# Residual rows in a seven-product down-projection: loaded by single tiles, a kept product, and their additions on GpSimd

## The reference

```python
def conv_ffn(h, w_up, conv_w, conv_b, w_down):
    u = causal_dwconv(h @ w_up, conv_w, conv_b)
    gate, val = jnp.split(u, 2, axis=-1)
    return (jax.nn.silu(gate) * val) @ w_down        # (1024, 2816) @ (2816, 1024)
...
x = x + concatenate([tok, xa]) @ w_out               # x_mid, kept in DRAM
x = x + conv_ffn(rms_norm(x, ffn_norm[i]), ...)      # the residual addition
h = rms_norm(x, mix_norm[i + 1])                     # what the next layer reads
```

## Time and profile before

| | |
|---|---|
| three runs | 2541.0, 2546.72, 2546.8 us |
| profiled execution, its own time | 2542.37 us |
| its span | 2540.6 us |
| PE busy | 2436.7 us (96%) |
| DVE busy | 1731.4 us (68%) |
| ACT busy | 1030.8 us (41%) |
| POOL busy | 194.6 us (8%) |
| mean DMA rate | 101 GB/s |

### The profile page before, as it was taken

The page is one execution under the profiler, slowest core; times in us unless marked ns, Lnnn a source line. Parts: engine busy times, 40 slices in busy tenths (PEclk is TensorE's granted clock), DMA queues, the critical chain, the costliest instruction groups (busy, mean ns, idle before and its releaser), DMA issues. The chain is left out here.

```text
span 2540.6 us, 32368 instructions
## 1 busy us (share of the span) xinstructions
PE 2436.7 (96%) x11700; PEld 2056.7 (81%) x11700; DVE 1731.4 (68%) x2934; ACT 1030.8 (41%) x2118; POOL 194.6 (8%) x269
## 2 busy tenths in 40 slices
PE   7999979999999998998999999998999999999898
PEld 7998757888888886777889889887888888887777
DVE  4432564479998987885553562463769989988895
ACT  6433443344444443335434442333334444443332
POOL 1010121000000000001212022122000000000000
PEclk9999988999999999999999999999999999999999
DMA  4231112222222247643102011212532222227653
GB/s 147 89 88 22 48 70 58 84 68 83 92 83 75 91 154 273 228 138 128 55 17 80 34 34 42 59 34 80 173 107 83 83 75 92 83 85 256 250 176 140
DMA packets 207349, 257.72 MB, mean 101 GB/s; under 512 B 38184, under 2 KB 141592, under 8 KB 207192
## 3 DMA queue, kind: packets, MB, share of 16 engines
q1 hardware_dynamic: 203032, 255.65, 30.6%
q10 hardware_dynamic: 4160, 0.02, 0.1%
HBM read 206.54 MB, written 49.09 MB: 101 GB/s over the span
## 5 line engine op out<-in xcount | busy, mean ns | idle before, releaser
L52 PE MATMUL psum<-f_T_lo 128*128 128x512 f32 x616 | 246.8, 401 | 31.0 <-DVE f_T_lo L654 29.3
L53 PE MATMUL psum<-f_T_lo 128*128 128x512 f32 x616 | 242.2, 393 | 0.0
L54 PE MATMUL psum<-f_T_lo 128*128 128x512 f32 x616 | 241.8, 393 | 0.0
L52 PE MATMUL psum<-w_hi,hT_hi 128*128 128x512 f32 x576 | 229.3, 398 | 3.9 <-DVE w_lo L1415 2.2
L54 PE MATMUL psum<-w_hi,hT_lo 128*128 128x512 f32 x576 | 226.3, 393 | 0.0
L53 PE MATMUL psum<-w_lo,hT_hi 128*128 128x512 f32 x576 | 226.1, 393 | 0.0
L52 PEld LDWEIGHTS psum<-f_T_lo 128*128 128x128 f32 x616 | 117.0, 190 | 68.2 <-DVE f_T_lo L654 40.9
L52 PEld LDWEIGHTS psum<-w_hi,hT_hi 128*128 128x128 f32 x576 | 124.8, 217 | 22.1 <-issue 3.5
L54 PEld LDWEIGHTS psum<-w_hi,hT_lo 128*128 128x128 f32 x576 | 125.0, 217 | 17.8
L53 PEld LDWEIGHTS psum<-w_lo,hT_hi 128*128 128x128 f32 x576 | 125.1, 217 | 16.6
L52 PE MATMUL psum<-hT_hi,f_up_hi 128*128 128x512 f32 x352 | 137.4, 390 | 0.4 <-DVE f_up_lo L593 0.4
(11 more groups left out here) (412 smaller groups left out, 6053.1 us busy)
## 6 DMA issues: line engine op xcount, KB each, us to landing
raw<-in_ffn_w_up_dram SPq DMA_DIRECT2D x88, 512.0 KB, 4.7
activations<-f_act SPq DMA_DIRECT2D x44, 512.0 KB, 2.6
f_up_pieces<-activations SPq DMA_DIRECT2D x38, 512.0 KB, 4.1
w_raw<-in_b_w_in_dram SPq DMA_DIRECT2D x18, 1024.0 KB, 6.1
f_up_pieces<-in_ffn_w_down_dram SPq DMA_DIRECT2D x20, 512.0 KB, 4.9
x_between<-XY SPq DMA_DIRECT2D x16, 512.0 KB, 5.3
XY<-x_between SPq DMA_DIRECT2D x4, 2048.0 KB, 15.4
f_up_pieces<-activations SPq DMA_DIRECT2D x28, 256.0 KB, 3.9
```

The costliest lines, as they stand in the source:

```text
L52: nc.tensor.matmul(out, lhs_hi, rhs_hi, start=start, stop=False)
L53: nc.tensor.matmul(out, lhs_hi, rhs_lo, start=False, stop=False)
L54: return nc.tensor.matmul(out, lhs_lo, rhs_hi, start=False, stop=stop)
```

## The change

- `load_rows` loads single tiles (512 KB): tiles 4 to 7 behind the loads of groups 5, 7, 9 and 10, tiles 0 to 3 behind those of 14, 16, 18 and 20. The store of the last activations moves from group 8 to group 12.
- POOL makes all additions of `k1` and `k7` to the rows: four 128x512 after step 0; four 128x512 and four 128x1024 (both halves of `x21` and `x22` with `k7` read twice) after `second_sums`; then four 128x512 that add the product which step 1 left in PSUM. That product is now copied out by ACT (`keep_second`, `p2_copy`, in the room of `conv_out`). `third_first` waits for all 16.
- `begin.low_parts` goes from DVE to POOL, between POOL's first four additions and the rest.
- `second_sums` and `third_second` each become four operations of 128x1024 in place of eight of 128x512.
- `taps_of` of the last chunk: value half behind the lows of group 3, gate half behind those of group 6; `silu` behind group 7, `multiply` behind group 8.
- `load_right` has four places instead of two and is issued up to four groups ahead. In step 3 the order of the norm's parts on ACT, DVE and PE is another, and four of its DVE operations come behind the last lows.

```diff
-Q, X11A, U, X11B, XU, X21P, X2P, X12F = 0, 4, 8, 16, 20, 32, 36, 44
+Q, U, X21P, X2P, X12F = 0, 4, 8, 12, 16
@@ raw_single
-                return up.pieces[:, 2 * (n % 2), :]
+                return (up.pieces[:, 2, :], up.pieces[:, 6, :], up.room[:, 0, FIRST], up.pieces[:, 0, :])[(n - LAST) % 4]
@@
+        p2_copy = [conv_out[i // 2][:, (i % 2) * HALF:(i % 2 + 1) * HALF] for i in range(4)]
...
+        def both(x):
+            return x.unsqueeze(1).broadcast_to([P, 2, HALF])
+        def halves(x):
+            return x.rearrange("p (h n) -> p h n", n=HALF)
@@ sync
-                sp.wait_ge(b_split, parts_until(LAST + g - 1))
-                sp.dma_start(raw_single(LAST + g), down_rows[2 * g + 1, :, SECOND]).then_inc(e_loaded[(LAST + g) % 2], 16)
-            def load_rows(i):
+                sp.wait_ge(b_split, parts_until(LAST + g - 3 if g >= 4 else LAST - 2 + max(0, g - 1)))
+                sp.dma_start(raw_single(LAST + g), down_rows[2 * g + 1, :, SECOND]).then_inc(e_loaded[g % 4], 16)
+            def load_rows(t):
                 sp.wait_ge(p_done, ALL)
-                sp.dma_start(X[:, 4 * i:4 * i + 4, :], ...)
+                sp.dma_start(X[:, t, :], x_mid[t * P:(t + 1) * P, :]).then_inc(x_loaded[t // 4], 16)
@@
-                if n == 8:
+                if n in (5, 7, 9, 10):
+                    load_rows({5: 4, 7: 5, 9: 6, 10: 7}[n])
+                if n == PAIRS + 1:
                     store_act(FC - 1)
-                    for i in (1, 0):
-                        load_rows(i)
+                if n in (14, 16, 18, 20):
+                    load_rows((n - 14) // 2)
@@ scalar
+            def keep_second():
+                act.wait_ge(prod_done, FC)
+                for i in range(4):
+                    act.wait_ge(out_done, 12 + i + 1)
+                    nc.scalar.activation(p2_copy[i], psum[:, 4 + i, :], ACT.Copy).then_inc(p2_copied, 1)
...
+                if n == 2 * PAIRS + 1:
+                    keep_second()
                 high_parts(n)
-                if n == 4:
+                if n == 7:
                     silu(FC - 1)
...
-                if begin and n == 2 * PAIRS + 1:
+                if begin and n == 2 * PAIRS + 3:
                     act.wait_ge(b_split, parts_until(2 * PAIRS))
                     begin.high_parts(act)
@@ vector
             def second_sums():
                 for i in range(4):
                     dve.wait_ge(out_done, 8 + i + 1)
-                    dve.wait_ge(added, X11A + 4)
-                    add(k1[:, i, :], k1[:, i, :], psum[:, i, :])
-                    add(k7[:, i, :], k7[:, i, :], psum[:, i, :])
-                for i in range(4):
-                    dve.wait_ge(out_done, 12 + i + 1)
-                    add(x11[i], x11[i], psum[:, 4 + i, :])
+                    dve.wait_ge(added, Q + 4)
+                    dve.wait_ge(rows_added, 4)
+                    k_both = halves(h_room[1][:, DH + i, :])
+                    add(k_both, k_both, both(psum[:, i, :]))
...
             def third_first():
                 for i in range(4):
-                    dve.wait_ge(added, XU + 12)
+                    dve.wait_ge(rows_added, 16)
...
+                pieces = X[:, i:i + 5:4, SECOND]
+                add(pieces, pieces, both(psum[:, 4 + i, :]))
...
-                if PAIRS + 2 <= n < PAIRS + 6:
-                    rows_first(n - PAIRS - 2)
-                if 2 * PAIRS + 2 <= n < 2 * PAIRS + 6:
-                    rows_second(n - 2 * PAIRS - 2)
-                if begin and n == 2 * PAIRS + 6:
-                    begin.low_parts(dve)
...
+            for g in range(5, PAIRS):
+                lows(LAST + g)
+                if norm and g in (5, 7, 9):
+                    norm.dve_gain(dve, (g - 5) // 2)
+                elif norm:
+                    norm.dve_low(dve, (g - 6) // 2)
@@ gpsimd
+            def row_add(out, x):
+                nc.gpsimd.tensor_tensor(out, out, x, ALU.add).then_inc(rows_added, 1)
+            pool.wait_ge(x_loaded[1], 64)
+            for i in range(4):
+                pool.wait_ge(k1_copied, i + 1)
+                row_add(x11[i], k1[:, i, :])
+            if begin:
+                begin.low_parts(pool)
+            pool.wait_ge(x_loaded[0], 64)
+            for i in range(4):
+                pool.wait_ge(added, U + i + 1)
+                row_add(x12[i], k1[:, i, :])
+                row_add(halves(X[:, i, :]), both(k7[:, i, :]))
+            for i in range(4):
+                pool.wait_ge(rows_added, 12)
+                pool.wait_ge(p2_copied, i + 1)
+                row_add(x11[i], p2_copy[i])
@@ tensor
+                elif step == 2 and which == 1:
+                    pe.wait_ge(p2_copied, i + 1)
...
-                if norm and 2 <= g < 6:
-                    turn_first(g - 2)
+                if norm and g in (2, 3, 4, 6):
+                    turn_first((2, 3, 4, 6).index(g))
```

More of the change, by code:

```diff
@@ L514, in _ @@
                 act.wait_ge(b_made, 3 * LAST)
-            for g in range(4):
+            for g in range(PAIRS):
+                if norm and g >= 4:
+                    if g == 4:
+                        square(0)
+                    if g == 5:
+                        scale(0)
+                        square(1)
+                    if g == 6:
+                        scale(1)
+                        norm.act_high(act, 0)
+                        square(2)
+                    if g == 7:
+                        scale(2)
+                    if g == 8:
+                        norm.act_high(act, 1)
+                        square(3)
+                    if g == 9:
+                        scale(3)
+                    if g == 10:
+                        norm.act_high(act, 2)
                 high_parts(LAST + g)
             if norm:
[L518 to L533, removed]
-                act.wait_ge(b_split, parts_until(LAST + PAIRS))
[L535 to L540, removed]
+                norm.act_high(act, 3)
+                act.wait_ge(b_split, parts_until(LAST + PAIRS))
+                square(4)
+                square(5)
+                scale(4)
+                scale(5)
+                square(6)
+                norm.act_high(act, 4)
+                scale(6)
+                square(7)
+                norm.act_high(act, 5)
+                scale(7)
+                norm.act_high(act, 6)
+                norm.act_high(act, 7)
         @block.vector
@@ L797, in _ @@
                 dve.wait_ge(act_stored, 16 * FC)
[L798 to L807 removed]
+            for g in range(5, PAIRS):
[4 more added lines that the diff above has]
+                    norm.dve_low(dve, (g - 6) // 2)
+            if norm:
+                norm.dve_gain(dve, 3)
+            for i in range(4):
                 rows_last(i)
+                if norm and i == 1:
+                    norm.dve_low(dve, 3)
             if norm:
[L810 to L814 removed]
+                for t in range(4, TT):
                     norm.dve_gain(dve, t)
                     norm.dve_low(dve, t)
[L818 to L820 removed]
+        @block.gpsimd
+        def _(pool):
+            def row_add(out, x):
[11 more added lines that the diff above has]
+                row_add(halves(X[:, i, :]), both(k7[:, i, :]))
+            for i in range(4):
+                pool.wait_ge(rows_added, 12)
+                pool.wait_ge(p2_copied, i + 1)
+                row_add(x11[i], p2_copy[i])
+            if norm:
                 for t in range(TT):
@@ L875, in wait_bank @@
                     pe.wait_ge(k1_copied, i + 1)
+                elif step == 2 and which == 1:
+                    pe.wait_ge(p2_copied, i + 1)
                 else:
-                    pe.wait_ge(added, {(1, 1): Q + i + 1, (2, 0): U + 2 * i + 2, (2, 1): X11B + i + 1, (3, 0): X21P + i + 1}[step, which])
+                    pe.wait_ge(added, {(1, 1): Q, (2, 0): U, (3, 0): X21P}[step, which] + i + 1)
             def turn_first(t):
-                pe.wait_ge(added, X2P + (8 if t % 2 else 4))
+                pe.wait_ge(added, X2P + (4 if t % 2 else 2))
                 norm.pe(pe, t)
@@ L908, in _ @@
                 last.then_inc(out_done, 1)
-                if norm and i == 2:
-                    pe.wait_ge(added, X12F + 2)
-                    norm.pe(pe, 4)
             if norm:
+                pe.wait_ge(added, X12F + 2)
+                norm.pe(pe, 4)
                 pe.wait_ge(norm.low, begin.TILES)
@@ L1349, in high_parts, with low_parts @@
             self.nc.scalar.activation(self.hi[kh], self.raw(kh), ACT.Copy).then_inc(self.high, 1)
-    def low_parts(self, dve):
+    def low_parts(self, pool):
         for kh in range(2):
-            dve.wait_ge(self.high, kh + 1)
-            self.nc.vector.tensor_tensor(self.lo[kh], self.raw(kh), self.hi[kh].bitcast(F32), ALU.subtract).then_inc(self.split, 1)
+            pool.wait_ge(self.high, kh + 1)
+            self.nc.gpsimd.tensor_tensor(self.lo[kh], self.raw(kh), self.hi[kh].bitcast(F32), ALU.subtract).then_inc(self.split, 1)
```

47 lines of the change are left out of this document (10 added, 37 removed).

## The result

The changed kernel takes 2550.56 us (median of 11 runs, 2546.62 to 2555.14), the kernel before 2542.95 on the same chip: a ratio of 1.0029, 95% interval 1.0019 to 1.0039 (the ratio is of the means, without one run of the kernel before that took 3465.47 us). That is 7.6 us or 0.3% slower where 2520 and faster were forecast. The profiled execution took 2553.04 us, its span 2551.2, which is 10.6 over the span before.

A forecast was written before the change was run, and what follows sets the result against it. PE is busiest, its down-projection waiting for DVE's low parts. Terms sum to -9.4 us in f0 and -14.9 in f1, together -24.3 on 2542.4: 2518, put at 2520 against the median; range 2502 to 2551.

The forecast's parts named there:

- loads, taps, POOL's start: Steps 0 and 1: row tiles -10.4 (f0), about -10.0 (f1); taps apart -1.8 per layer; POOL's first additions +1 per layer.
- step 2: POOL's additions relieving DVE in step 2: f0 +5.8 us because `third_first` comes late, f1 -2.6 us.
- step 3: Four load places and new norm order: f0 -4 us (bounds 0 and -9), f1 -1.5 us.
- Who gets in?: Step 2, POOL against DVE: POOL gets in where DVE waits, so work is conserved; main case 2520, chance 0.50.
- Rows 8 to 10: Earlier profile rows: DVE operations of 0.28 us took up to 2.36 beside POOL; one POOL operation of 0.55 took 1.75.
- Rival 2: Step 2: POOL and DVE take turns, a waiting POOL operation following each DVE operation; 2548 to 2552 us, chance 0.28.
- The loads: Step 0: row loads by tiles remove PE's 8.7 us hole and its clock loss; f0 -10.4, f1 about -10.0.
- rival 3: Row tiles still hold the group loads up, eight at up to 1.3 us: +5 per layer, 2530 us, chance 0.09.
- The taps: Step 0: two pairs of taps set three groups apart no longer make PE wait; -1.8 us in each layer.
- POOL's price alone: Durations of POOL's additions: about 1.26 us for 128x512, an estimate, and 2.37 for 128x1024.
- third_first: f0, end of step 2: it waits for all 16 POOL additions and is 8.9 us late, PE with it.
- The clock behind the holes: After a long PE hole matmuls restart at the lower clock, costing 1.7 us.

The follow-up runs named there:

- pool_paced: Changed kernel with the same POOL work, but each addition waiting for the low parts of a group of its own, `begin.low_parts` last: 2527.33 us, ratio 0.9929.
- tile_loads_alone: Kernel before with only the row loads by single tiles and the activation store behind group 12: 2528.66 us, ratio 0.9939.
- pool_one_column: Changed kernel with each of POOL's 16 row additions per layer cut to the first column of its operands: 2519.55 us, ratio 0.9900.
- taps_as_before: Changed kernel with all additions on DVE and the taps, silu and multiply at their old places: 2513.94 us; run once more on another chip, 2515.9.

## Why the prediction was wrong

Step by step, in us per layer, from the counts of lost time (the loads, taps and step 1 of the prediction are one stretch):

| | predicted f0, f1 | count after less before f0, f1 |
|---|---|---|
| loads, taps, POOL's start | -11.2, -10.8 | -4.1, -5.2 |
| step 2 | +5.8, -2.6 | +11.4, +10.4 |
| step 3 | -4, -1.5 | -3.9, -1.7 |
| sum | -9.4, -14.9 | +3.4, +3.5 |

- **The step that failed** is the answer to "Who gets in?": "POOL gets in where DVE waits. Then the work must be conserved." With a full queue POOL does not wait for gaps; it and DVE alternate, instruction by instruction, and POOL's are the longer ones (1.1 and 2.2 us against 0.60). That the work of both fits into step 2 was beside the point, because PE needs the low parts group by group: in f1 a debt of 16 us that could have been paid over ten groups was called in within the eleven DVE operations from 2441.86 on, the work of two groups. `pool_paced` shows exactly this: the same work spread out loses 11.0 and 10.5 us less in step 2. Step 2 alone is 5.6 us (f0) and 13.0 (f1) off, 18.6 of the 31.2 that the sum missed. The other 12.7 lie ahead of step 2: by the counts 3.5 in the loads, 3.6 in the taps, 3.6 in POOL's first additions, and some 2 that no single run explains.
- **Rows 8 to 10 held both answers.** Three of the four operations of the earlier trace rows were held, each by one POOL operation, as the turns say. I set above them one POOL operation of 0.55 us that took 1.75. That it waited out two DVE operations was read rightly: in the changed kernel the same operation takes 1.62 at 1150.56, and one of 0.19 us takes 2.00 at 1154.49, beside three low parts that begin behind it and go at 0.68. But it was a single POOL operation, and said nothing about a POOL queue that always has the next one ready. The chance of 0.28 for the turns was too low for a rival that the longer row supported.
- **Rival 2's own numbers** came out close: a hole of 14 us in f1 (measured 12.04), and 2548 to 2552 in all (2550.56). In f0 it had 1.4, 8.2, 7.2 and 2.5, measured 5.5 and 5.5 us and one of 0.75. The holes came from writing both queues' operations in order, not from their sums. That the total fits so well is in part luck: its step 2 is +17.9 and +12.0 us where +11.4 and +10.4 were counted, 8 too much, and its loads, taps and step 1 are 10 too good.
- **The loads: right mechanism, wrong size.** The 10 us wait and the long hole went. Predicted were -20.4; `tile_loads_alone` gives -15.6, its counts -8.8 and -8.1. In step 0 it is -10.3 and -9.2, nearly as priced; the term put at nothing was step 1, which loses 1.5 and 1.1 us more. What is left is rival 3 in small: tiles behind which DVE waits 1.4 to 2.3 us. Rivals 2 and 3 came true together, a case that the prediction had not priced.
- **The taps: wrong.** -3.6 predicted, nothing measured (2516.14 and 2514.64). "Nothing shows" had rested on 2 us by which low parts may be late, and did not count that DVE's sums start behind a load and stand in front of the low parts.
- **POOL's price alone was right**: 1.26 and 2.37 us were the estimates, 1.29 and 2.39 is what the unheld ones take in `pool_paced`. In the burst they took 1.79 to 1.99 and 2.96 on average. What its first four additions cost ahead of step 2 was put at 1 us per layer; `pool_one_column` against the changed kernel says 3.0 in f0 and 2.6 in f1. In f0 2.2 of it are the two low parts held at 1003.79 and 1005.49; in f1 three low parts were held, and the wait before step 1 is 3.26 us.
- **`third_first`** was to be 8.9 us late in f0 behind POOL. In a burst POOL is done early, and this wait does not show; step 3 loses the same 7.6 us up to its last three groups with POOL's additions as with those of one column.
- **Step 3** came out as said, in sum and for each layer: -3.9 and -1.7.
- The clock behind the holes was priced from the earlier trace rows and came out alike: the first matmuls take 0.79 us and then follow at 0.43, and 0.90 and 0.92 stand as clocks in the two windows.

Not settled: why a POOL operation at times waits out several DVE operations in a row (1.75 us in the earlier trace rows, 6.26 in `pool_paced`) where one of the burst comes in after each; and the 3.7 us of span outside the down-projections. A difference of 4 us before the first down-projection also stands between profiles whose work there is the same (it ends at 938.75 in `taps_as_before` and at 943.30 in the kernel with the additions on DVE), so it may be no effect of the change.

## What to carry to other kernels

Before work is moved from DVE to GpSimd, ask of the operations on both sides whether they read their operands from SBUF: if both do, a full queue on GpSimd alternates with DVE one for one and delays it at once, against the deadline of the next group and not of the stage. Then leave the work on DVE, or tie each GpSimd operation to a point where DVE has slack. And test the parts of a combined change singly: here the loads by tiles, the new step 3 and the kept product, with all additions on DVE, make 2514 to 2521 us, about 1.1% under the kernel before, and beat both kernels.

## What the runs showed of the hardware

- Against a DVE addition or subtraction of 128x512 with both operands in SBUF (0.69 us), a GpSimd addition of 128x512 holds it for 1.1 us, of 128x1024 for 2.2, of 128x256 for 0.53, a copy of 128x512 for 0.4, and a fill for nothing. With one operand in PSUM DVE was not held (`second_sums`, 4.61 us for four).
- In the bursts above two full queues alternate, one instruction each: 2.87, 1.77, 2.85, 1.75 us in POOL's own order of sizes. Cutting GpSimd's instructions in two lets DVE through twice as often, and here that gave 5 us back (2550.56 to 2545.28; by the ratios to the kernel before 0.3%).
- Outside a burst a GpSimd operation can wait out a whole run of DVE operations: 6.26 us for one of 2.39 behind five, 2.00 for one of 0.19 behind four, the first of each already running.
- A fill of 128x512 on GpSimd takes 0.53 us, less than half of an addition by itself (1.28), a copy 0.61. The groups by line in the kernel with fills:

```profile
L830 POOL MEMSET XY<- 128x512 f32 x24 | 11.9, 528 | 1032.6 <-ACT h_room_lo L468 971.3 <-DVE h_room_lo L687 61.2
L830 POOL MEMSET XY<- 128x1024 f32 x8 | 7.6, 954 | 0.0
```
